# Half of the FFN output columns by seven 2x2 block products in place of eight

## What is computed

```python
a, b = jnp.split(h @ w_in, 2, axis=-1)      # w_in: 1024 x 5632
y = (jax.nn.silu(a) * b) @ w_out            # w_out: 2816 x 1024
x = x + 0.5 * y                             # first block
x = x + 0.5 * rms_norm_2(y, norm_post)      # second model's layers
```

## Time and profile before

| what | value |
|---|---|
| median of 3 runs | 1726.48 us (1726.48 to 1726.56) |
| the profiled execution | 1726.28 us |
| its span, first to last instruction | 1724.5 us |
| granted TensorE clock, mean | 1.000 |
| PE busy | 1717.4 us, 100% |
| DVE busy | 1072.7 us, 62% |
| ACT busy | 918.9 us, 53% |
| DMA | 328.58 MB, mean 191 GB/s |

### The profile page before, as it was taken

How to read it: one execution, slowest core, us unless ns; L and a number is a source line. 1 busy time by engine, 2 the same in 40 slices (tenths; PEclk the granted TensorE clock), 3 DMA queues, 4 the chain that set the end, 5 groups by cost and what they waited for, 6 DMA issues and landing times.

```text
span 1724.5 us, 31112 instructions
## 1 busy us (share of the span) xinstructions
PE 1717.4 (100%) x12536; PEld 1586.4 (92%) x12536; DVE 1072.7 (62%) x1523; ACT 918.9 (53%) x1258; POOL 34.5 (2%) x60
## 2 busy tenths in 40 slices
PE   9999999999999999999999999999999999999998
PEld 9999888999999999999999999899999899989997
DVE  6555787655665566557677555755574667775555
ACT  6444677434454346577746444644464577664443
POOL 0000120000000000000000000000000000000000
PEclk9999999999999999999999999999999999999999
DMA  9655533655665555463355555655555553446552
GB/s 341 237 193 193 183 112 149 229 185 193 223 226 187 189 194 202 177 220 139 133 197 197 193 187 197 230 205 193 189 203 188 181 195 136 162 160 228 185 194 96
DMA packets 48415, 328.58 MB, mean 191 GB/s; under 512 B 5584, under 2 KB 5840, under 8 KB 10192
## 3 DMA queue, kind: packets, MB, share of 16 engines
q1 hardware_dynamic: 45504, 316.93, 51.3%
q10 hardware_dynamic: 2832, 10.54, 1.7%
HBM read 326.39 MB, written 1.05 MB: 190 GB/s over the span
## 4 chain that ended last, share of the span: by engine, by line
PE 99%; issue 0%; DVE 0%; ACT 0%; DVEq 0%; POOLq 0%; POOL 0%
PE work L1888 20%; PE work L1890 20%; PE work L1889 20%; PE acc L1890 8%; PE acc L1889 8%; PE acc L1888 8%; PE work L2129 4%; PE work L1993 3%; PE acc L2197 1%; PE acc L2251 1%; PE work L1978 1%; PE acc L2225 1%; PE acc L2215 0%; PE work L2379 0%; PE work L2259 0%; PE work L1950 0%
## 5 line engine op out<-in xcount | busy, mean ns | idle before, releaser
L1262 DVE TENSOR_TENSOR lo<-raw,hi 128x2048 fp32r<-128x2048 f32 x267 | 611.1, 2291 | 308.3 <-ACT hi L711 307.9
L711 ACT ACTIVATE hi<-raw 128x2048 fp32r<-128x2048 f32 x267 | 511.2, 1915 | 370.7 <-PE work L1890 346.8
L1888 PE MATMUL work<-xT_hi,hi 128*128 128x256 f32 x2464 | 685.4, 278 | 0.0
L1889 PE MATMUL work<-xT_lo,hi 128*128 128x256 f32 x2464 | 681.2, 276 | 0.0
L1890 PE MATMUL work<-xT_hi,lo 128*128 128x256 f32 x2464 | 681.1, 276 | 0.0
L1888 PEld LDWEIGHTS work<-xT_hi,hi 128*128 128x128 f32 x2464 | 462.6, 188 | 4.5 <-issue 1.7
L1889 PEld LDWEIGHTS work<-xT_lo,hi 128*128 128x128 f32 x2464 | 463.2, 188 | 2.4
L1890 PEld LDWEIGHTS work<-xT_hi,lo 128*128 128x128 f32 x2464 | 462.7, 188 | 0.0
L1890 PE MATMUL acc<-hi,hT_lo 128*128 128x512 f32 x480 | 189.1, 394 | 0.0
L1889 PE MATMUL acc<-lo,hT_hi 128*128 128x512 f32 x480 | 188.2, 392 | 0.0
L1888 PE MATMUL acc<-hi,hT_hi 128*128 128x512 f32 x480 | 186.4, 388 | 0.0
(11 more groups left out here) (357 smaller groups left out, 2108.0 us busy)
## 6 DMA issues: line engine op xcount, KB each, us to landing
raw<-stream SPq DMA_DIRECT2D x295, 1024.0 KB, 4.8
mem_in<-mem ACTq DMA_DIRECT2D x3, 1024.0 KB, 5.2
post<-post ACTq DMA_DIRECT2D x6, 512.0 KB, 4.4
raw<-stream SPq DMA_DIRECT2D x4, 512.0 KB, 9.3
memT_raw<-mem2T ACTq DMA_DIRECT2D x2, 1024.0 KB, 7.4
xT_raw<-xT SPq DMA_DIRECT2D x4, 256.0 KB, 5.4
raw<-stream SPq DMA_DIRECT2D x4, 256.0 KB, 6.0
x<-x SPq DMA_DIRECT2D x2, 512.0 KB, 9.2
```

The costliest lines, as they stand in the source:

```text
L711: nc.scalar.activation(dst, raw[:, s, :], ACT.Copy).then_inc(hi_ready, 1)
L1262: nc.vector.tensor_tensor(lo[:, s, :], raw[:, s, :], hi[:, s, :].bitcast(F32), ALU.subtract).then_inc(lo_ready, 1)
L1888: nc.tensor.matmul(dst, a_hi, b_hi, start=start, stop=False)
L1889: nc.tensor.matmul(dst, a_hi, b_lo, start=False, stop=False)
```

## The change

In chunks 1 to 8 of each FFN the first 512 of the 1024 output columns are no longer made by plain products. Tokens by hidden channels are a 2x2 grid of 128 x 128 blocks (a11 to a22), hidden channels by those 512 columns a 2x2 grid of 128 x 256 blocks (b11 to b22). Eight block products with 256 moving columns (four matmul triples of 512) are replaced by seven in Winograd's form of Strassen's scheme, 21 matmuls of 256 columns in place of 12 of 512. The other 512 columns stay as they were.

- DVE makes four sums of token blocks (`token_sums`, 128 x 128 each) after `gated`, and four of weight blocks (`weight_sums`, 128 x 256 each, from `raw`) before the last `split_low` of the chunk. ACT makes the high part of each set (128 x 512 and 128 x 1024), DVE the low part. DVE waits on its own semaphore between dependent sums, and for ACT before each low part.
- PE, `seven_out`: the plain half first, then two of the seven products, then a wait for the low parts of the sums (`sums_lo`), then the other five. Products go to parts of `work` banks 2 and 3 and of `acc` banks 0 and 2. The four parts in `work` run on over the eight chunks.
- In chunk 9 (`plain_chunk`) ACT copies `work` banks 3 and 2 to `seven` in SBUF and DVE combines them with four additions (`seven_joined`).
- At the end of the FFN DVE adds `seven` to the bank of the first columns (`join`, one instruction for each token tile, 128 x 512), and ACT's squares and DVE's residual of these columns read the joined sum in SBUF and wait for it.
- On PE chunks 2 and 9 leave the loop and are written out. `mem_norm_turned` moves from ahead of chunk 10's `chunk_in` to between its two units, and `mem_scaled` on DVE from ahead of `scaled_a` of chunk 10 to behind it.

```diff
+SEVEN = CHUNKS - 3
@@ ScalarE, loop body of an FFN
                 def chunk(j):
+                    done = 2 * SEVEN * ffn_at(sec, k)
                     split_high(sec, u0 + 2, j)
                     silu(j)
                     split_high(sec, u0 + 3, j)
                     high_h(j, u0 + 1, j)
+                    act.wait_ge(sums_made, done - 1 + j * 2)
+                    nc.scalar.activation(h_sums_hi, h_sums, ACT.Copy).then_inc(sums_hi, 1)
+                    split_high(sec, u0 + 4, j)
+                    act.wait_ge(sums_made, done + j * 2)
+                    nc.scalar.activation(w_sums_hi, w_sums, ACT.Copy).then_inc(sums_hi, 1)
@@ plain_chunk, before its last split_high
+                    for b in (1, 0):
+                        nc.scalar.activation(pair(seven, b), work[:, 2 + b, :], ACT.Copy).then_inc(seven_copied, 1)
@@ post_sums
+                    if r != 1 and c == 0:
+                        act.wait_ge(joined, joined_at(sec, r, i))
@@ VectorE
+                def token_sums(j):
...
+                    dve.wait_ge(h_ready, c0 + j + 1)
+                    nc.vector.tensor_tensor(s1, a21, a22, ALU.add).then_inc(sum_step, 1)
+                    nc.vector.tensor_tensor(s3, a11, a21, ALU.subtract)
+                    dve.wait_ge(sum_step, first - 3)
+                    nc.vector.tensor_tensor(s2, s1, a11, ALU.subtract).then_inc(sum_step, 1)
+                    dve.wait_ge(sum_step, first - 2)
+                    nc.vector.tensor_tensor(s4, a12, s2, ALU.subtract).then_inc(sums_made, 1)
...
                 def chunk(j):
                     scaled_a(j, u0 - 1, j)
                     split_low(sec, u0 + 2, j)
                     gated(j, u0, j)
+                    token_sums(j)
                     split_low(sec, u0 + 3, j)
                     low_h(j, hT_hi, hT_lo)
+                    dve.wait_ge(sums_hi, done - 1 + j * 2)
+                    nc.vector.tensor_tensor(h_sums_lo, h_sums, h_sums_hi.bitcast(F32), ALU.subtract).then_inc(sums_lo, 1)
+                    weight_sums(j)
                     split_low(sec, u0 + 4, j)
+                    dve.wait_ge(sums_hi, done + j * 2)
+                    nc.vector.tensor_tensor(w_sums_lo, w_sums, w_sums_hi.bitcast(F32), ALU.subtract).then_inc(sums_lo, 1)
...
                 last = CHUNKS - 1
+                scaled_a(last, u0 - 1 + 3 * last)
                 if mem_gain is not None:
                     mem_scaled(sec)
-                scaled_a(last, u0 - 1 + 3 * last)
...
+            def join(sec, r, n, i):
+                sums_ready(dve, sec, r, n, i, 0)
+                y = whole_sum(r, i, 0)
+                nc.vector.tensor_tensor(y, acc[:, 2 * i, :], y, ALU.add).then_inc(joined, 1)
...
             def post_residual(sec, r, p, scale, i, eps, between=None):
                 scaled = []
+                if r != 1:
+                    join(sec, r, (L_MEM if r == 0 else L_UNITS) - 1, i)
@@ TensorE
+                def seven_out(n, j, trip, first=False, final=False):
...
+                    pe.wait_ge(hTlo_ready, c0 + j + 1)
+                    parts_ready(sec, n, trip)
+                    for i in range(TT):
+                        for f in range(2):
+                            w = slice(D * f + 512, D * f + 1024)
+                            a = ((a11, a12), (a21, a22))[i][f]
+                            multiply(acc[:, 2 * i + 1, :], a, (hi[:, s, w], lo[:, s, w]))
+                    multiply(work[:, 2, 0:T], a11, b11, start=first)
+                    multiply(acc[:, 0, 0:T], a12, b21)
+                    pe.wait_ge(sums_lo, 2 * SEVEN * ffn_at(sec, k) + j * 2)
+                    multiply(acc[:, 0, T:2 * T], s4, b22)
+                    multiply(acc[:, 2, 0:T], a22, t4)
+                    multiply(work[:, 2, T:2 * T], s2, t2, stop=final)
+                    multiply(work[:, 3, 0:T], s3, t3, start=first)
+                    multiply(work[:, 3, T:2 * T], s1, t1, stop=final).then_inc(unit_used, 1)
...
-                with pe.Fori(2, CHUNKS - 1) as j:
+                chunk_in(u0 - 1, 2, 2)
+                seven_out(u0 + 1, 1, 2, first=True)
+                with pe.Fori(3, CHUNKS - 2) as j:
                     chunk_in(u0 - 1, j, j)
-                    chunk_out(u0 + 1, j - 1, j)
+                    seven_out(u0 + 1, j - 1, j)
+                j = CHUNKS - 2
+                chunk_in(u0 + 3 * j - 1, j, 0)
+                seven_out(u0 + 3 * j + 1, j - 1, 0, final=True)
                 j = CHUNKS - 1
-                if mem:
-                    mem_norm_turned(sec)
-                chunk_in(u0 + 3 * j - 1, j, 0)
+                chunk_in(u0 + 3 * j - 1, j, 0, between=(lambda: mem_norm_turned(sec)) if mem else None)
```

More of the change, by code:

```diff
@@ L562, in entry, with ffn_at, joined_at, whole_sum @@
             return 0 if sec.layer is None else 1 + 2 * sec.layer + (k != 0)
+        def ffn_at(sec, k):
+            return sec.at(2, 2, k)
+        def joined_at(sec, r, i):
+            return 2 * ffn_at(sec, r // 2) + i + 1
+        def whole_sum(r, i, c):
+            return seven[:, 2 * i:2 * i + 2, :].rearrange("p q t -> p (q t)") if r != 1 and c == 0 else acc[:, 2 * i + c, :]
         def tile_step(sec, k, i, r):
@@ L850, in ffn @@
                     middle()
-                    with act.Fori(CHUNKS // 2, CHUNKS - 1) as j:
+                    with act.Fori(CHUNKS // 2, CHUNKS - 2) as j:
                         chunk(j)
@@ new lines, in chunk @@
+                def chunk(j):
+                    done = 2 * SEVEN * ffn_at(sec, k)
+                    scaled_a(j, u0 - 1, j)
+                    split_low(sec, u0 + 2, j)
+                    gated(j, u0, j)
+                    token_sums(j)
+                    split_low(sec, u0 + 3, j)
+                    low_h(j, hT_hi, hT_lo)
+                    dve.wait_ge(sums_hi, done - 1 + j * 2)
+                    nc.vector.tensor_tensor(h_sums_lo, h_sums, h_sums_hi.bitcast(F32), ALU.subtract).then_inc(sums_lo, 1)
+                    weight_sums(j)
+                    split_low(sec, u0 + 4, j)
+                    dve.wait_ge(sums_hi, done + j * 2)
+                    nc.vector.tensor_tensor(w_sums_lo, w_sums, w_sums_hi.bitcast(F32), ALU.subtract).then_inc(sums_lo, 1)
@@ new lines, in seven_joined, with plain_chunk @@
+                def seven_joined():
+                    p1, p6, p7, p5 = (seven[:, b, :] for b in range(4))
+                    dve.wait_ge(seven_copied, 2 * ffn_at(sec, k) + 2)
+                    step.link(nc.vector.tensor_tensor(p6, p1, p6, ALU.add))
+                    step.link(nc.vector.tensor_tensor(p7, p6, p7, ALU.add))
+                    nc.vector.tensor_tensor(p6, p6, p5, ALU.add)
+                    step.link(nc.vector.tensor_tensor(p5, p7, p5, ALU.add))
+                def plain_chunk(j):
@@ L2079, in ffn, with chunk_in @@
                 c0 = sec.at(2 * CHUNKS, 2 * CHUNKS, k * CHUNKS)
-                def chunk_in(n, j, trip):
+                def chunk_in(n, j, trip, between=None):
                     for part in range(2):
+                        if between and part == 1:
+                            between()
                         pe.wait_ge((first_read, h_ready)[part], c0 + j)
```

63 lines of the change are left out of this document (54 added, 9 removed).

## The result

| | median (runs) | ratio to before, 95% interval |
|---|---|---|
| before | 1726.3 us (6) | |
| changed | 1736.66 us (6), 1735.13 to 1737.39 | 1.0061 [1.0050, 1.0072] |

The forecast was 1715.1 us. The changed kernel is 10.4 us slower than before, where 11.4 us faster was forecast. Its profiled execution took 1735.13 us, with a span of 1733.3 at a granted clock of 0.999.

What follows compares the result with a forecast made beforehand. PE was taken to bound the kernel, busy for the whole span; 17.6 us saved in the product loop less 6.2 us lost at the ends gave 11.4 us, so 1726.48 to 1715.1 us, with an 8-in-10 range of 1709.5 to 1721.0.

Steps and rivals of the forecast that it cites:

- PE bounds the kernel, a matmul taken away counts in full: Whole kernel: PE is 99% of the chain; product loop saves 0.37 us a chunk, 17.6 us in 48 chunks.
- The pace of the matmuls: Product loop: the 21 new 256-column matmuls keep chunk_in's 113.5 ns each; at 118.6 the gain would be 12.5 us.
- The rival that the small products are slow: Product loop: changing PSUM part every three matmuls costs 118.6 ns a matmul, time 1720.2 us; chance 0.12.
- DVE and ACT hide what is added: Product loop: DVE rises to 13.7 us a chunk, ACT to 8.5, against 16.03; nothing reaches PE.
- The ends: Ends of the FFNs and program: join and squares make PE late, 6.2 us in all, bounds 1 and 13.
- DVE as the bound: Product loop: rival that DVE's additions pass 7.1 us a chunk; 1737.7 us at a 16.5 us chunk; chance 0.05.
- a falling clock: New PE stalls: rival that each of three brings some 3 us of 1.2 GHz pace, 9 us, 1724 us; chance 0.04.
- covered ends: Ends of the FFNs: rival that slack hides the added steps, loss 1 us, time 1709.9 us; chance 0.12.
- The sum: Whole kernel: 17.6 - 6.2 = 11.4 us gained, new span 1713.1 us, new median 1715.1 us.

Runs made afterwards that it cites:

- aligned: The changed kernel with the tiles of all sums moved so that every operand pair lies 192 bytes apart modulo 512; 1728.99 us, ratio 1.0021.
- after_even: The changed kernel, sums at their old addresses, with one 512-column matmul of each seven_out split into two of 256; 1718.99 us, ratio 0.9962.
- aligned_22: Against aligned: no 512-column matmul split, one 256-column matmul of the last of the seven products split into two of 128; 1735.97 us, ratio 1.0059.

## Why the prediction was wrong, step by step

- **PE bounds the kernel, a matmul taken away counts in full.** Right: the fast-pace sum fell by 17.7 us, forecast 17.6, and seven_out takes 5.13 us where the pace is fast (aligned).
- **The pace of the matmuls.** This is the step that failed: "I see no reason for less than 113.5 with the same shape, so that is the other bound, and I take it", and with it the unsaid term that the matmuls which stay keep their pace, put at nothing without a reason. In its place about half of the matmuls of 256 columns ran at 117.8 in place of 113.3 ns, an excess 20.4 us greater than before. Where the sums lie accounts for 7.7 us of the time (`aligned`). One split matmul a chunk, with the sums left where they were, gave back 17.7 us (after_even). So most of the loss hangs on the form of the stream, and why one form holds the slow pace and another does not stays open. Both paces were in the trace of before: in the slow stretch of the earlier trace rows (11.39 us, read as 118.6 ns each) the first matmul behind the transposes takes 201 ns and the other 95 take 117.8 ns. I read it as a property of that place.
- **The rival that the small products are slow.** Its price for one matmul, 5.1 ns, was near the 4.4 measured, and its extent was wrong. It priced 21 slow matmuls a chunk, 5.1 us in all. In the trace the pace, once slow, was mostly kept through the next two chunks, so half of the stream paid: an excess of 25.4 us, 20.4 more than before. Its time of 1720.2 was 16.5 us short. The reason that it named, the change of PSUM part, was wrong.
- **DVE and ACT hide what is added.** Right. A chunk of 16.56 us has 12.92 us of DVE (8.96 + 3.97 in the rows above; forecast 13.7) and 8.50 of ACT (forecast 8.5). The sums of 128 x 128 took 0.29 us, 128 x 256 0.42, the low part of 128 x 1024 1.22. No wait reached PE in the loop.
- **The ends.** Forecast 0.3, 1.9, 2.0, 0.6 and 1.1, measured 0.59, 1.82, 1.83, 0.52 and 1.09 us. One had another cause: after the block's first FFN PE waited for `lo` of the next unit and not for x. split_low stood behind the joins in DVE's queue, and I had followed only x. The tail behind the last matmul grew by 0.04 us, forecast 0.2.
- **DVE as the bound, a falling clock, covered ends.** None came. The granted clock was 0.999 over the span with stalls of 1.8 us. The clock rival's "some 3 us" a stall and its 9 us came from no row, and the clock behind both stalls of 1.8 us is 1.00 (2.4 GHz).
- **The sum.** With the excess of before (5.0) in place of 25.4 the changed kernel's span would be 1733.3 - 20.4 = 1712.9, and 1713.1 was forecast. All versions with seven products but aligned_22 have a span less excess of 1707.2 to 1708.7 us. The range missed because it held no case in which untouched matmuls change their pace.

## What to carry to other kernels

When a matmul stream is the bound, check the pace of the matmuls that a change does not touch, start to start, before blaming those that it adds: here 4.4 ns on half of the stream turned a gain of about 10 us into a loss of 10. Give a new operand tile the offset modulo 512 bytes of the tile whose role it takes (7.7 us here, and nothing once a matmul was split), and try other orders of the same work (one split moved the changed kernel by 17.7 us). In a prediction, a slow stretch in the trace of before is a state that the change could spread, and should be priced over everything behind it.

## What the hardware showed

- The distance modulo 512 bytes between the two operands' tiles moves the pace of float32 matmuls of 256 columns here: 113.3 ns at best at 192, and at 64 in after_even; over whole kernels 118.7 at 128 and 119.9 at 0 and 256. With 192 the slow pace of 117.8 ns still occurs. One number in the placing was worth 48 us or more. The Trainium skill ("TensorE: Matmul & The Clock Gate", Step-by-step: what each phase is for) says that TensorE reads the moving operand and the weights through two independent ports, so that loading weights takes no bandwidth from a running matmul. These runs don't show which reads meet, but they do show that the two places matter together.
- The slow pace persists, over 131 matmuls in a row in `aligned`. Around its end there is mostly one step of 121 to 124 ns, 8 to 11 over the fast pace (121 at the first matmul of chunk_in in `aligned`, 124 at the end of a22 by t4 in the changed kernel). The trace does not show its mechanism.
- Two matmuls of 128 columns inside such a stream cost 0.11 us more than the one of 256 that they replace.
